# Nine of v's matmuls right behind the first product's first step; the row scale formed and copied elsewhere in DVE's order

## The reference

```python
h = _rms(x, g_mix[l])
z = h @ w_in[l]
za, zu, zv, zq, zg = jnp.split(z, SPLITS, axis=-1)
ya = jax.nn.gelu(_s5(za, a_re[l], a_im[l], log_dt[l], ...))
...
yb = _sgu(zu, zv, g_sgu[l], beta_sgu[l], w_s[l], b_s[l]) @ w_b_out[l]
yc = _mem_xattn(zq, mem, g_mem[l], w_kv[l]) @ w_c_out[l]
```

## Time and profile before

| | us |
|---|---|
| Three runs, median (lowest, highest) | 768.41 (768.12, 768.69) |
| The profiled execution | 768.33 |
| Its span | 766.6 |
| TensorE busy | 758.3 (99%) |
| DVE busy | 552.5 (72%) |
| ACT busy | 355.4 (46%) |
| POOL busy | 314.6 (41%) |

### The profile page before, as it was taken

The page is one execution under the profiler, slowest core; times in us unless marked ns, Lnnn a source line. Parts: engine busy times, 40 slices in busy tenths (PEclk is TensorE's granted clock), DMA queues, the critical chain, the costliest instruction groups (busy, mean ns, idle before and its releaser), DMA issues.

```text
span 766.6 us, 9762 instructions
## 1 busy us (share of the span) xinstructions
PE 758.3 (99%) x3562; PEld 629.0 (82%) x3562; DVE 552.5 (72%) x752; ACT 355.4 (46%) x529; POOL 314.6 (41%) x169
## 2 busy tenths in 40 slices
PE   8999999999999999999999999999999999999997
PEld 7788887788888888888888888888888888888886
DVE  6999997684848484246767787777787677836687
ACT  6796567643535333634343423232323333434554
POOL 4456655233333333444444444444444354830000
PEclk9999999999999999999999999999999999999999
DMA  7744333022222443222233866666668567768853
GB/s 273 301 147 131 117 98 112 30 91 83 81 85 68 126 144 104 83 93 100 83 111 99 272 196 228 217 217 191 201 204 285 176 218 228 264 229 279 293 201 125
DMA packets 42371, 126.17 MB, mean 165 GB/s; under 512 B 4192, under 2 KB 6368, under 8 KB 40544
## 3 DMA queue, kind: packets, MB, share of 16 engines
q1 hardware_dynamic: 42192, 125.45, 49.1%
q10 hardware_dynamic: 144, 0.26, 0.1%
HBM read 107.08 MB, written 18.61 MB: 164 GB/s over the span
## 4 chain that ended last, share of the span: by engine, by line
PE 91%; ACT 3%; DVE 3%; DMA 1%; issue 1%; SPq 0%; POOL 0%; ACTq 0%
PE bank L1641 24%; PE bank L1643 24%; PE bank L1642 24%; PE bank L2005 4%; PE bank L2007 4%; PE bank L2006 4%; ACT uc L656 1%; DVE s5p L1015 1%; PE bank L1882 1%; PE bank L1757 1%; PE bank L1774 1%; DMA xT<-xt_dram 1%; ACT w_hi L596 1%; DVE tab_tmp L1015 1%; DVE h_lo L1020 1%
## 5 line engine op out<-in xcount | busy, mean ns | idle before, releaser
L535 POOL TENSOR_TENSOR w_lo<-raw,w_hi 128x1024 fp32r<-128x1024 f32 x90 | 218.1, 2424 | 300.7 <-ACT w_hi L596 300.7
L596 ACT ACTIVATE w_hi<-raw 128x1024 fp32r<-128x1024 f32 x112 | 118.8, 1060 | 310.9 <-PE bank L1643 306.3
L1641 PE MATMUL bank<-h_hi,w_hi 128*128 128x512 f32 x608 | 238.5, 392 | 0.2 <-POOL w_lo L540 0.2
L1643 PE MATMUL bank<-h_hi,w_lo 128*128 128x512 f32 x608 | 236.7, 389 | 0.0
L1642 PE MATMUL bank<-h_lo,w_hi 128*128 128x512 f32 x608 | 236.6, 389 | 0.0
L1641 PEld LDWEIGHTS bank<-h_hi,w_hi 128*128 128x128 f32 x608 | 114.2, 188 | 24.3 <-issue 1.0
L1643 PEld LDWEIGHTS bank<-h_hi,w_lo 128*128 128x128 f32 x608 | 114.1, 188 | 23.9
L1642 PEld LDWEIGHTS bank<-h_lo,w_hi 128*128 128x128 f32 x608 | 114.2, 188 | 23.7 <-issue 0.5
L540 POOL TENSOR_TENSOR w_lo<-raw,w_hi 128x512 fp32r<-128x512 f32 x48 | 67.2, 1420 | 52.4 <-ACT w_hi L596 46.0
L1015 DVE TENSOR_TENSOR mix<-mix 128x512 f32<-128x512 f32 x44 | 47.6, 1083 | 13.1 <-DMA mix<-w_dram 11.9
L1015 DVE TENSOR_TENSOR lo<-raw,hi 128x1536 fp32r<-128x1536 f32 (+1 forms) x19 | 32.8, 1732 | 24.8 <-ACT hi L925 24.6
(11 more groups left out here) (328 smaller groups left out, 1384.6 us busy)
## 6 DMA issues: line engine op xcount, KB each, us to landing
raw<-w_dram SPq DMA_DIRECT2D x112, 512.0 KB, 3.4
mix<-w_dram SPq DMA_DIRECT2D x11, 1024.0 KB, 8.0
mix_dram<-mix SPq DMA_DIRECT2D x11, 1024.0 KB, 6.3
raw<-w_dram SPq DMA_DIRECT2D x30, 256.0 KB, 4.3
raw<-mix_dram SPq DMA_DIRECT2D x26, 256.0 KB, 3.8
half_dram<-odd SPq DMA_DIRECT2D x11, 256.0 KB, 8.3
second<-half_dram SPq DMA_DIRECT2D x3, 768.0 KB, 6.0
raw<-mix_dram SPq DMA_DIRECT2D x3, 768.0 KB, 4.2
```

What stands on the lines that cost most here:

```text
L535: nc.gpsimd.tensor_tensor(w_lo[:, s, :], raw[:, s, :], fv(w_hi[:, s, :]), ALU.subtract).then_inc(w_ready, 1)
L596: nc.scalar.activation(w_hi[:, slot, :], raw[:, slot, :], ACT.Copy).then_inc(w_rounded, 1)
L1641: mm(out, a[0], b[0], start=first, stop=False)
L1643: return mm(out, a[1], b[0], start=False, stop=last)
```

## The change

Half of v's first weight tile (its first 512 columns, one input block) gets buffers of its own (`raw_v`, `v_hi`, `v_lo`) and a load of its own, third among the weight and x loads. ACT rounds it behind the first part of x, POOL subtracts behind tile 0's first half, and the nine matmuls of v's first block go behind step 0 of the first product instead of behind step 7. Tile 4 as a whole is still loaded and split for the rest. Its rounding on ACT moves from behind the root to a place ahead of the fourth token square, and its load on SP moves ahead of the fourth `xtok` load. On DVE the row scale is formed behind the first table step instead of inside the second, and `rstd` is copied behind the second instead of behind the third. Six semaphores become three to make room for three new ones.

```diff
@@ block.sync @@
             for k in range(4):
                 load_first(k // 2, k % 2)
                 load_x(k)
+                if k == 0:
+                    sp.dma_start(raw_v[:, :], w_d[T_ZV, :, 0:WB]).then_inc(v_loaded, 16)
...
-            for t in range(4):
+            for t in range(3):
                 sp.dma_start(xtok[:, t, :], xtok_d[:, t, :]).then_inc(xtok_loaded[t], 16)
             next_weights(4)
+            sp.dma_start(xtok[:, 3, :], xtok_d[:, 3, :]).then_inc(xtok_loaded[3], 16)
@@ block.gpsimd @@
                     low_half(t, j).then_inc(done, 1)
+                    if t == 0 and j == 0:
+                        pool.wait_ge(v_rounded, 1)
+                        nc.gpsimd.tensor_tensor(v_lo[:, :], raw_v[:, :], fv(v_hi[:, :]), ALU.subtract
+                                                ).then_inc(v_ready, 1)
@@ block.scalar @@
                 round_x(k)
+                if k == 0:
+                    act.wait_ge(v_loaded, 16)
+                    nc.scalar.activation(v_hi[:, :], raw_v[:, :], ACT.Copy).then_inc(v_rounded, 1)
...
             for t in range(4):
+                if t == 3:
+                    round_weights(T_ZV)
                 act.wait_ge(xtok_loaded[t], 16)
                 token_square(xtok, t, t)
             act.wait_ge(tok_sq, 4)
             root(tstd[:, :], tssq[:, 0:4]).then_inc(tok_std, 1)
-            round_weights(T_ZV)
@@ block.vector @@
             table_step(1)
-            table_step(2, x_scale)
+            x_scale()
+            table_step(2)
+            dve.wait_ge(wide_done, 1)
+            V.tensor_copy(rstd[:, :], bank[7][:, :]).then_inc(rstd_ready, 1)
             table_step(4)
-            dve.wait_ge(wide_x, 1)
-            V.tensor_copy(rstd[:, :], bank[7][:, :]).then_inc(rstd_ready, 1)
             dve.wait_ge(rstd_ready, 1)
@@ block.tensor @@
-            for k in range(KD):
+            za_step(0)
+            x_hi, x_lo = h(0)
+            pe.wait_ge(v_rounded, 1)
+            for c in range(3):
+                mm(bank[4 + c][:, :], x_hi[:, c * P:(c + 1) * P], v_hi[:, :], start=True, stop=False)
+            for c in range(3):
+                mm(bank[4 + c][:, :], x_lo[:, c * P:(c + 1) * P], v_hi[:, :], start=False, stop=False)
+            pe.wait_ge(v_ready, 1)
+            for c in range(3):
+                mm(bank[4 + c][:, :], x_hi[:, c * P:(c + 1) * P], v_lo[:, :], start=False, stop=False)
+            for k in range(1, KD):
                 za_step(k)
...
-            pe.wait_ge(w_half, T_ZV + 1)
-            zv_step(0, range(3))
-            pe.wait_ge(diag_x, 1)
-            wide_rows(7, xdiag[:, :, :], T, wide_x)
+            pe.wait_ge(diag, 1)
+            wide_rows(7, xdiag[:, :, :], T, wide_done)
```

More of the change, by code:

```diff
@@ L216, in build @@
         std = at("std", o_s + (4 * C_BRE + 63) // 64 * 64, [P, T])
+        raw_v = at("raw_v", o_f + 2048, [P, WB])
+        v_hi = at("v_hi", o_f + 4096, [P, WB], R)
+        v_lo = at("v_lo", o_f + 6144, [P, WB], R)
         mstd = at("mstd", o_f, [P, M])
@@ L265, in build @@
         w_used = sem("w_used")
+        v_loaded, v_rounded, v_ready = sems("v_loaded v_rounded v_ready")
         X_PARTS = ((0, 1), (1, 2), (2, 3), (3, 4), (4, 6), (6, 8))
@@ L277, in build @@
         norms = {n: dict(zip(keys, sems(" ".join(f"{n}_{k}" for k in keys)))) for n, keys in NORM_KEYS.items()}
-        tok_sq, tok_std, diag_x, diag_m, wide_x, wide_m, rstd_ready, mrstd_ready = sems(
-            "tok_sq tok_std diag_x diag_m wide_x wide_m rstd_ready mrstd_ready")
+        tok_sq, tok_std, diag, wide_done, rstd_ready, mrstd_ready = sems(
+            "tok_sq tok_std diag wide_done rstd_ready mrstd_ready")
         za_taken, zv_taken, zq_taken, k_taken, v_taken, zu_scaled, zu_ready = sems(
@@ L286, in build @@
         pt_done, pt_act, pt_dve, pv_done, o_hi_s, o_lo_s = sems("pt_done pt_act pt_dve pv_done o_hi_s o_lo_s")
-        dt_ready, ang_ready, trig_ready = sems("dt_ready ang_ready trig_ready")
+        ang_ready, trig_ready = sems("ang_ready trig_ready")
         j1_g, j1_th, j1_merge = sems("j1_g j1_th j1_merge")
@@ L623, in _ @@
             act.wait_ge(vec_loaded, 16)
-            nc.scalar.activation(s5p[:, 0, :], small[:, C_LDT:C_LDT + 16], ACT.Exp).then_inc(dt_ready, 1)
+            nc.scalar.activation(s5p[:, 0, :], small[:, C_LDT:C_LDT + 16], ACT.Exp).then_inc(trig_ready, 1)
             for k in range(4):
@@ L1027, in _ @@
             dve.wait_ge(vec_loaded, 16)
-            dve.wait_ge(dt_ready, 1)
+            dve.wait_ge(trig_ready, 1)
             go(tt(XR, are, DT, ALU.mult))
@@ L1048, in _ @@
                 low_x(k)
-            dve.wait_ge(trig_ready, 1)
+            dve.wait_ge(trig_ready, 2)
             go(tt(ARE, MAG, CS, ALU.mult))
@@ L1110, in table_sum, with table_step @@
                 return tt((cosT, sinT)[j][:, :, n:2 * n], q[2 * j], q[2 * j + 1], (ALU.subtract, ALU.add)[j])
-            def table_step(n, scale=None):
+            def table_step(n):
                 table_half(n, (0, 1))
@@ L1115, in table_step @@
                 link(table_sum(n, 1))
-                if scale:
-                    scale()
                 turn_squared(ER, EI, ER, EI)
@@ L1129, in x_scale @@
             def x_scale():
-                token_scale(4, 1, tstd[:, :], trstd[:, :], xdiag[:, :, :], diag_x)
+                token_scale(4, 1, tstd[:, :], trstd[:, :], xdiag[:, :, :], diag)
             table_step(1)
-            table_step(2, x_scale)
+            x_scale()
+            table_step(2)
+            dve.wait_ge(wide_done, 1)
+            V.tensor_copy(rstd[:, :], bank[7][:, :]).then_inc(rstd_ready, 1)
             table_step(4)
-            dve.wait_ge(wide_x, 1)
-            V.tensor_copy(rstd[:, :], bank[7][:, :]).then_inc(rstd_ready, 1)
             dve.wait_ge(rstd_ready, 1)
@@ L1144, in _ @@
                 low_tile(norms["m"], m_hi, m_lo, memf, C_GMEM, k)
-            token_scale(2, 2, mtstd[:, :], mtrstd[:, :], mdiag[:, :, :], diag_m)
+            token_scale(2, 2, mtstd[:, :], mtrstd[:, :], mdiag[:, :, :], diag)
             bre, bim, cre, cim = (grid(c0) for c0 in (C_BRE, C_BIM, C_CRE, C_CIM))
@@ L1173, in _ @@
             times([c[:, 0, :, :] for c in cpow], (cre, cim), ARE, AIM, True, 1)
-            dve.wait_ge(wide_m, 1)
+            dve.wait_ge(wide_done, 2)
             V.tensor_copy(mrstd[:, :], bank[3][:, 0:M]).then_inc(mrstd_ready, 1)
@@ L1729, in _ @@
                 if t == 3:
-                    pe.wait_ge(diag_m, 1)
+                    pe.wait_ge(diag, 2)
                     pe.wait_ge(za_taken, KB)
-                    wide_rows(3, mdiag[:, :, :], M, wide_m)
+                    wide_rows(3, mdiag[:, :, :], M, wide_done)
                 for j in range(2):
```

## The result

The changed kernel takes 769.56 us (median of 22 runs, 768.95 to 770.96), the kernel before 768.48 beside it (22 runs, 767.56 to 770.48): 1.08 us more, ratio 1.0015, 95% interval 1.0008 to 1.0022. It is slower, by less than the 0.2% that the forecast took for no change. The profiled execution took 769.02 (span 767.3), 0.69 over that of the kernel before; it is one of the changed kernel's faster ones.

What follows compares the result with a forecast made beforehand. Bound: the chain to TensorE's wait at 61.42 us, through ACT's series that starts when the fourth `uT` is written. `uT` 1.9 us later, TensorE's 0.24 gain lost: 768.33 + 1.9 = 770.2 us, range over cases 767.9 to 771.2.

Steps and rivals of the forecast that it cites:

- The sum's path: Third table step held by POOL, fourth `uT` late, ACT's series from 36.91 us starts 1.9 us later, TensorE's wait grows.
- Nine matmuls: TensorE after the first step: v's nine matmuls take 2.04 us, ending at 11.11 us.
- tile 4's rounding: ACT, ahead of the fourth token square: starts at 24.97 us, ends at 26.0; POOL's two halves run 26.1 to 28.7.
- the root: ACT's token root behind the fourth token square: `tstd` ready at 28.7 us, not 26.27.
- DVE held by tile 4's pair: POOL's pair at 26.1 us holds DVE's table work to 30.2; `xdiag` ends at 31.1, bounds 30.4 and 31.6.
- Tile 5 at 33.2: v's 256 KB costs the queue 0.62 us; tile 5 taken at 33.2 us, bounds 32.5 and 33.4.
- It meets the third table step.: POOL's pair for tile 5, beginning at 34.3 us, holds DVE's third table step, ending it at 35.6 or 36.9.
- the first of the prediction's own signs of being wrong: In the profile after: third table step over before POOL's first half of tile 5 begins.
- rival 1: Third table step escapes POOL; `uT` ends between 36.8 and 37.5 us, time 768.2 to 769.0, no change; chance 0.28.
- rival 2: TensorE's gain stays: `uT` at 36.2 us, ACT 0.6 sooner, floor 36.02 at tile 6; 767.7 us; chance 0.08.
- The catch's price: POOL's tile 5 pair holding the third table step makes `uT` 1.3 or 2.5 us later; 1.9 taken.
- rival 3: Worse: DVE held at both places for both halves, TensorE waiting for tile 5; `uT` 39.7, 771.2 us; chance 0.05.

Runs made afterwards that it cites:

- the table step moved: Changed kernel with the third table step put behind the memory rows' scale on DVE; median 769.74 us, ratio 1.0016 to the kernel before.
- the second execution: The changed kernel, unaltered, run and profiled once more; profiled execution 768.64 us, median 769.01, ratio 1.0011 to the kernel before.
- the orders alone: Changed kernel without v's early half tile, its nine matmuls behind the first product again; median 769.96 us, ratio 1.0019 to the kernel before.

## Why the prediction was right in its sign and wrong in its cause

- *Direction and range.* Slower, as forecast, and 769.56 lies in 767.9 to 771.2; but 0.64 us under the 770.2 forecast, and under the 0.2% on the far side of which stood the larger chance. The sum's path, a `uT` that ends at 38.1 or 39.4, did not happen (36.68), so that the time lies in the range is luck.
- *Nine matmuls, tile 4's rounding, the root* came as worked out: 2.04 us for the nine; rounding at 25.21 for 24.97; POOL's pair at 26.35 for 26.1; root at 28.62 to 28.92 for 28.7.
- *DVE held by tile 4's pair*: shown, but the pair began 0.25 us later than taken and DVE was at the tables sooner, so `xdiag` ended at 30.39 instead of 31.1, at the early bound of 30.4.
- *Tile 5 at 33.2* is the mis-sized term: its rounding began at 33.86, and with the same loads at 33.42 and, with the table step moved, 35.00. The prediction counted the exchange on SP only for the fourth xtok transfer ("1.9 us at the queue's rate"); for tile 5 it added v's 256 KB alone. The exchange itself costs the queue 0.2 to 2 us from the third xtok transfer to tile 5, as the landings with it and without it show, and cover takes that away. What v's bytes add isn't clear from single executions: the third xtok transfer landed at 21.8 to 23.4 us in the eleven with v, at 22.2 to 22.5 in the three without.
- *The step that failed*: "It meets the third table step." This is the first of the prediction's own signs of being wrong. With `xdiag` 0.7 sooner and tile 5 up to 0.7 later, the step was over 0.84 us before POOL's pair, in the second execution 0.15 us before it (34.41 against 34.56). These are rival 1's conditions. Rival 1 then priced only `uT`, and had no change; the ACT series behind tile 5 (rounding, two token squares, root: 3.4 us) was in the earlier trace rows at 32.54 to 36.02, with 0.89 us to spare, and a tile 5 that is 1.3 late uses that up. That floor was used once, in rival 2, and not for a late tile 5.
- *The catch's price*, 1.3 or 2.5 us, was right: where it happens, `uT` ends at 39.41 and 39.12.
- *TensorE's wait for tile 5* stood in rival 3 as a part of the worst case. It came without the rest, 1.33 us, and ate the 0.94 that the moved matmuls had won; it isn't in the chain that sets the end, which runs through ACT from 33.86 to 60.

That the slowest executions of the changed kernel (770 to 771) have a late tile 5 and not the catch is argued, not shown: the kernel that can't have the catch is as slow and spreads as widely, but none of those executions was traced, and the second traced one escaped the catch by only 0.15 us.

## What to carry to other kernels

On a queue that is served in order, a transfer's place matters beyond its bytes: what lies between a load that waits for its slot and the work ahead of it is cover, and moving it away can cost as much as several hundred KB (here 1.1 us at about 420 GB/s). When two late things meet (a transfer and an engine's step), work out both orders of arrival, and give each its price down to the engine that sets the end. A relation that holds in every trace (here time = tile 10's start + 707) turns a 0.1% question about medians into a reading of two rows.

## What the runs showed of the hardware

In the kernels with the exchange nothing stands on SP's queue behind the third xtok transfer until tile 4's slot is free. There the queue was slow for some 3 to 4 us, although in the changed kernel tile 4's load was issued 2.7 us before that transfer landed; 512 KB more in between took the slow stretch away. The DMA's busy share hardly shows it. In the changed kernel the slices at 305, 265 and 295 GB/s have busy digits of 8, 9 and 9, those at 410 to 440 behind them 9: only GB/s tells them apart. Each kernel here has another slow stretch between 12 and 18 us, before included; there the busy digit falls in places too. Why the queue gets slow stays open.

A MEMSET passes beside POOL where a `TENSOR_TENSOR` of its size doesn't. In the kernel of the orders alone, with POOL's pair of two halves:

```profile
25.80 2.55 POOL L546 TENSOR_TENSOR w_lo<-raw,w_hi 128x512 fp32r<-128x512 f32 x2 [3.51 <-ACT w_hi L602]
```

```profile
25.84 1.28 DVE L1022 TENSOR_TENSOR s5p<-s5p 128x16 f32<-128x16 f32 x1
27.04 0.16 DVE L1091 COPY s5p<-s5p 128x16 f32<-128x16 f32 x1
27.29 0.07 DVE L1125 MEMSET cosT<- 128x16 f32 x1
27.32 0.07 DVE L1126 MEMSET sinT<- 128x16 f32 x1
27.42 0.98 DVE L1022 TENSOR_TENSOR tab_tmp<-cosT,s5p 128x16 f32<-128x16 f32 x1
```

Both memsets lie inside the second half (from about 27.1 to 28.35), and the product behind them is held to its end. This is what the rule named in the prediction, the Trainium skill's *SBUF — State Buffer*, "SBUF: two separate sides", would have; the trace agrees, with 0.07 us each.
